# A two-layer mixer kernel: the narrow projection panel between the two halves of z, and its small products ahead of the head sums

## The reference, cut to what matters

```
n = rms_norm(h, norm_mix[l])
q, k, v, z, a, b, bq, bk, bv, iq, ik, iw = split(n @ w_in[l])      # 3408 columns
q, k, v = silu(causal_dwconv(q, k, v))
q = l2_norm(q) * 128 ** -0.5 ; k = l2_norm(k)                       # 4 heads of 128
g = -exp(a_log) * softplus(a + dt_bias) ; beta = sigmoid(b)
# chunked gated delta rule: decays from cumsum(g), one triangular solve per chunk
o = rms_norm(o, norm_g) * silu(z)
# second branch: bq, bk, bv attend to keys chosen by an indexer made of iq, ik (64 wide) and iw (8 wide)
ik = rope(rms_norm(ik))
```

## Time and profile before

| | |
|---|---|
| median of three runs | 1634.32 us (1628.2 to 1634.47) |
| profiled execution | 1631.81 us, its span 1630.0 us |
| mean granted clock of PE | 0.99 of full speed |
| busy share of the span | PE 97%, DVE 72%, ACT 56%, POOL 4% |
| shares of the chain that ended last | PE 82%, DVE 10%, ACT 4%, issue 2%, DMA 2% |
| the piece of the change, layer 0 | about 64 to 98 us |
| the piece of the change, layer 1 | about 527 to 558 us |

### The profile page before, as it was taken

How to read it: one execution, slowest core, us unless ns; L and a number is a source line. 1 busy time by engine, 2 the same in 40 slices (tenths; PEclk the granted TensorE clock), 3 DMA queues, 4 the chain that set the end, 5 groups by cost and what they waited for, 6 DMA issues and landing times.

```text
span 1630.0 us, 34719 instructions
## 1 busy us (share of the span) xinstructions
PE 1584.6 (97%) x12673; PEld 1546.5 (95%) x12673; DVE 1178.5 (72%) x1929; ACT 905.0 (56%) x1419; POOL 71.2 (4%) x62
## 2 busy tenths in 40 slices
PE   8997999999999989999999999999999999999998
PEld 7987989999999879899999989999999999999998
DVE  8778777866559689688666668888756746678863
ACT  5764465655446745556555555665645455566642
POOL 3101001000010101000000000000000000000000
PEclk9999999999999999999999999999999999999999
DMA  6643235455555432265665554566655544546663
GB/s 208 202 118 95 92 103 180 157 178 180 165 174 156 143 102 93 71 207 170 210 201 178 163 182 129 156 200 186 182 181 187 168 134 151 181 151 196 187 184 113
DMA packets 272207, 261.41 MB, mean 160 GB/s; under 512 B 20009, under 2 KB 270533, under 8 KB 272115
## 3 DMA queue, kind: packets, MB, share of 16 engines
q1 hardware_dynamic: 270547, 256.15, 50.9%
q0 software_dynamic: 1376, 3.87, 0.8%
q10 hardware_dynamic: 192, 0.14, 0.0%
HBM read 256.70 MB, written 3.42 MB: 160 GB/s over the span
## 4 chain that ended last, share of the span: by engine, by line
PE 82%; DVE 10%; ACT 4%; issue 2%; DMA 2%; SPq 1%; DVEq 0%; ACTq 0%
PE lin L551 22%; PE lin L554 22%; PE lin L559 22%; PE aux L899 6%; PE lin L899 3%; PE lin L605 3%; DVE wL L538 2%; PE lin L576 1%; ACT wH L529 1%; PE lin L636 1%; DVE cT L2075 1%; DMA stage<-in_w_gate 1%; DVE nT L2530 1%; DVE nL L2535 1%; DVE prod L2193 0%
## 5 line engine op out<-in xcount | busy, mean ns | idle before, releaser
L529 ACT ACTIVATE wH<-stage 128x1024 fp32r<-128x1024 f32 x488 | 493.5, 1049 | 479.8 <-PE lin L554 333.3
L538 DVE TENSOR_TENSOR wL<-stage,wH 128x1024 fp32r<-128x1024 f32 x488 | 580.2, 1231 | 141.1 <-PE lin L559 82.6
L551 PE MATMUL lin<-nH,wH 128*128 128x256 f32 (+2 forms) x2256 | 560.7, 287 | 3.3 <-DVE rawT L2146 2.4
L554 PE MATMUL lin<-nL,wH 128*128 128x256 f32 (+2 forms) x2256 | 555.4, 285 | 0.0
L551 PEld LDWEIGHTS lin<-nH,wH 128*128 128x128 f32 x2256 | 426.3, 189 | 6.8 <-issue 4.9
L554 PEld LDWEIGHTS lin<-nL,wH 128*128 128x128 f32 x2256 | 427.3, 189 | 1.1 <-issue 0.7
L559 PE MATMUL lin<-nH,wL 128*128 128x256 f32 (+2 forms) x2256 | 295.0, 283 | 0.5 <-DVE wL L538 0.5
L559 PEld LDWEIGHTS lin<-nH,wL 128*128 128x128 f32 x2256 | 281.4, 188 | 0.7 <-DVE wL L538 0.7
L551 PE MATMUL lin<-aH,wH 128*128 128x256 f32 (+1 forms) x704 | 172.3, 284 | 0.0
L554 PE MATMUL lin<-aL,wH 128*128 128x256 f32 (+1 forms) x704 | 172.2, 284 | 0.0
L551 PEld LDWEIGHTS lin<-aH,wH 128*128 128x128 f32 x704 | 132.8, 189 | 0.0
(11 more groups left out here) (416 smaller groups left out, 2200.9 us busy)
## 6 DMA issues: line engine op xcount, KB each, us to landing
stage<-in_w_up SPq DMA_DIRECT2D x88, 512.0 KB, 4.6
stage<-in_ffn_w_up SPq DMA_DIRECT2D x88, 512.0 KB, 4.3
stage<-in_w_in SPq DMA_DIRECT2D x52, 512.0 KB, 4.7
stage<-in_w_down SPq DMA_DIRECT2D x40, 512.0 KB, 3.7
stage<-in_ffn_w_down SPq DMA_DIRECT2D x40, 512.0 KB, 4.3
stage<-in_w_gate SPq DMA_DIRECT2D x32, 512.0 KB, 4.2
stage<-in_even_w_in SPq DMA_DIRECT2D x24, 512.0 KB, 4.6
stage<-in_w_out SPq DMA_DIRECT2D x16, 512.0 KB, 4.3
```

What stands on the lines that cost most here:

```text
L529: nc.scalar.activation(wH[:, s, ks, 0:n], stage[:, s, ks, 0:n], ACT.Copy).then_inc(sem["whi"], 1)
L538: nc.vector.tensor_tensor(wL[:, s, ks, 0:n], stage[:, s, ks, 0:n], wH[:, s, ks, 0:n].bitcast(F32), ALU.subtract).then_inc(sem["wlo"], 1)
L551: mm = nc.tensor.matmul(banks[b][0:rows_, 0:width], wH[:, s, k, cols], xh, start=start and n == 0, stop=False)
L554: mm = nc.tensor.matmul(banks[b][0:rows_, 0:width], wH[:, s, k, cols], xl, start=False, stop=False)
```

## The change

SP, ACT, DVE and PE take z's second half and the narrow panel in the other order: m0+4 slot 0 is z's first half, m0+4 slot 1 the narrow panel (PE writes bank 2 now), m0+5 slot 0 z's second half, m0+5 slot 1 the key panel as before. PE does `ta` and `sik` ahead of the eight head sums, behind z's second half. `JOBS` has the names in the new order. ACT copies the narrow panel between z's halves, and its `w_in(5, ...)` for z's second half begins with the split of panel m0+6 slot 0, whose place behind the `root`s is given up. `turned` on ACT stands in front of the `root_log`s.

```
--- before.py
+++ after.py
@@ -182,7 +182,7 @@
 
 
 JOBS = (
-    ["ms1"] + [f"ssq{h}" for h in range(4)] + ["ta"] + [f"ssk{h}" for h in range(4)] + ["sik", "gc", "tv"]
+    ["ms1", "ta", "sik"] + [f"ssq{h}" for h in range(4)] + [f"ssk{h}" for h in range(4)] + ["gc", "tv"]
     + ["gb0", "bb0", "gb1", "bb1"] + ["kk0", "qk0", "kk1", "qk1"] + ["gb2", "bb2", "kk2", "qk2"]
     + [f"ix0{e}" for e in range(2)] + [f"ix1{e}" for e in range(4)]
     + [f"sbq{h}" for h in range(4)] + ["sbk"] + ["Y1_4", "Y2_4"] + [x for b in range(3) for x in (f"kt{b}", f"vt{b}")]
@@ -726,11 +726,12 @@
                 with sp.Fori(1 if l == 0 else 0, 3) as i:
                     for s in range(2):
                         load(sp, m0 + i, s, whole(w_in, l, DC, i * 512 + s * PANEL))
-                for i, col in ((3, C_IQ), (4, 3 * 512)):
-                    for s in range(2):
-                        load(sp, m0 + i, s, whole(w_in, l, DC, col + s * PANEL))
-                load(sp, m0 + 5, 0, [(k0, k0 + 4, w_in[:, l * DC + k0:l * DC + k0 + 4, C_IK:IN_COLS]) for k0 in (0, 4)], IN_COLS - C_IK)
-                sp.dma_start(stage[:, 0, :, IN_COLS - C_IK:NARROW], w_in[:, l * DC:(l + 1) * DC, C_AB:C_AB + 8]).then_inc(sem["ab_in"], 16)
+                for s in range(2):
+                    load(sp, m0 + 3, s, whole(w_in, l, DC, C_IQ + s * PANEL))
+                load(sp, m0 + 4, 0, whole(w_in, l, DC, 3 * 512))
+                load(sp, m0 + 4, 1, [(k0, k0 + 4, w_in[:, l * DC + k0:l * DC + k0 + 4, C_IK:IN_COLS]) for k0 in (0, 4)], IN_COLS - C_IK)
+                sp.dma_start(stage[:, 1, :, IN_COLS - C_IK:NARROW], w_in[:, l * DC:(l + 1) * DC, C_AB:C_AB + 8]).then_inc(sem["ab_in"], 16)
+                load(sp, m0 + 5, 0, whole(w_in, l, DC, 3 * 512 + PANEL))
                 load(sp, m0 + 5, 1, whole(w_in, l, DC, C_BK))
                 for s in range(2):
                     load(sp, m0 + 6, s, whole(w_in, l, DC, C_BQ + s * PANEL))
@@ -957,11 +958,12 @@
                 multiply_second(pe, m0 + 1, r0 + 1, halves(0, nH, nL), T,
                                 lambda pair: (sem["nh"], at("nh", l, pair + 1)), lambda pair: (sem["nl"], at("nl", l, pair + 1)))
                 w_in(1, 1)
-                for i in (2, 3, 4):
+                for i in (2, 3):
                     for s in range(2):
                         w_in(i, s)
-
-                multiply(pe, m0 + 5, 0, r0 + 5, [(0, slice(0, NARROW), [(k, nH[:, k, :], nL[:, k, :]) for k in range(DC)])], T, rows_=NARROW)
+                w_in(4, 0)
+                multiply(pe, m0 + 4, 1, r0 + 4, [(2, slice(0, NARROW), [(k, nH[:, k, :], nL[:, k, :]) for k in range(DC)])], T, rows_=NARROW)
+                w_in(5, 0)
                 pe.wait_ge(sem["par_in"], 2 * DEPTH)
                 pe.wait_ge(sem["sq_heads"], at("sq_heads", l, 2))
 
@@ -970,18 +972,18 @@
                         name = f"ss{'qk'[h // 4]}{h % 4}"
                         mm(begin(name, l)[:, 0:T], ones, sqh[:, h, :]).then_inc(filled(name), 1)
 
-                def turned(name, x, p0, n, free):
+                def turned(name, x, p0, n, free, rnd):
                     ps = begin(name, l)
-                    pe.wait_ge(free, r0 + 6)
+                    pe.wait_ge(free, rnd)
                     for b in range(3):
                         t = nc.tensor.transpose(ps[0:TB[b][1], b * n:(b + 1) * n], x[p0:p0 + n, tok(b)], ident[p0:p0 + n, p0:p0 + n])
                     t.then_inc(filled(name), 1)
 
-                head_squares(0)
-                turned("ta", iab, IDX_DIM, 16, lin_read[0])
-                head_squares(4)
+                turned("ta", iab, IDX_DIM, 16, lin_read[2], r0 + 5)
                 pe.wait_ge(sem["sq_ik"], at("sq_ik", l, 1))
                 mm(begin("sik", l)[:, 0:T], ones, sq_ik[:, :]).then_inc(filled("sik"), 1)
+                head_squares(0)
+                head_squares(4)
                 w_in(5, 1)
                 pe.wait_ge(sem["tables_in"], 32)
                 pe.wait_ge(sem["gt"], at("gt", l, 1))
@@ -990,7 +992,7 @@
                     n = TB[b][1]
                     t = mm(ps[0:n, 4 * b:4 * b + 4], const("upto", n, n), gg[0:n, b, :])
                 t.then_inc(filled("gc"), 1)
-                turned("tv", bvT, 0, P, lin_read[3])
+                turned("tv", bvT, 0, P, lin_read[3], r0 + 6)
 
                 def gate(i, slots=(0, 1)):
                     for s in slots:
@@ -1494,9 +1496,9 @@
 
                 act.preload_act_table_set(SILU)
 
-                def w_in(i, to, func=Copy, slots=(0, 1), n=T):
+                def w_in(i, to, func=Copy, slots=(0, 1), n=T, cols=PANEL):
                     for s in slots:
-                        split_hi(act, m0 + i + 1, s)
+                        split_hi(act, m0 + i + 1, s, n=cols)
                         act.wait_ge(sem["panel_done"], 2 * (m0 + i) + s + 3)
                         for c in range(2):
                             b = 2 * s + c
@@ -1534,16 +1536,21 @@
 
                 w_in(3, lambda b: rawT[:, 20 + b:21 + b, META:T], slots=(0,), n=SEQ)
                 queries_swapped(0)
-                w_in(3, lambda b: rawT[:, 20 + b:21 + b, META:T], slots=(1,), n=SEQ)
                 act.wait_ge(sem["ab_in"], at("ab_in", l, 16))
-                for s in range(2):
-                    split_hi(act, m0 + 5, s, n=PANEL if s else NARROW)
-                    act.wait_ge(sem["panel_done"], 2 * (m0 + 4) + s + 3)
-                    for b in range(2 * s, 2 * s + 2):
-                        f(zT[:, b, :], lin[b][:, 0:T], Silu).then_inc(lin_read[b], 1)
-                    if s == 0:
-                        group_silu(2)
-                        queries_swapped(1)
+                w_in(3, lambda b: rawT[:, 20 + b:21 + b, META:T], slots=(1,), n=SEQ, cols=NARROW)
+                w_in(4, lambda b: zT[:, b:b + 1, :], Silu, slots=(0,))
+                group_silu(2)
+                queries_swapped(1)
+                act.wait_ge(sem["panel_done"], 2 * (m0 + 4) + 4)
+                f(iab[IDX_DIM:NARROW, :], lin[2][IDX_DIM:NARROW, 0:T], Copy)
+                for p0 in (0, IDX_DIM):
+                    t = f(ikr[p0:p0 + IDX_DIM, :], lin[2][0:IDX_DIM, 0:T], Copy)
+                t.then_inc(lin_read[2], 1)
+                act.sem_inc(lin_read[3], 1)
+                split_hi(act, m0 + 5, 1)
+                act.wait_ge(lin_read[2], r0 + 5)
+                f(sq_ik[:, :], ikr[:, :], Square).then_inc(sem["sq_ik"], 1)
+                w_in(5, lambda b: zT[:, 2 + b:3 + b, :], Silu, slots=(0,))
                 act.preload_act_table_set(EXP_LN)
 
                 def root_log(names, to, scale, h0=0):
@@ -1555,24 +1562,15 @@
                     act.wait_ge(*read(last, l))
                     f(to[:, :, :], to[:, :, :], Exp, scale=-0.5, bias=bias_).then_inc(sem["rn"], 1)
 
-                act.wait_ge(sem["panel_done"], 2 * (m0 + 5) + 3)
-                f(iab[IDX_DIM:NARROW, :], lin[0][IDX_DIM:NARROW, 0:T], Copy)
-                for p0 in (0, IDX_DIM):
-                    t = f(ikr[p0:p0 + IDX_DIM, :], lin[0][0:IDX_DIM, 0:T], Copy)
-                t.then_inc(lin_read[0], 1)
-                act.sem_inc(lin_read[1], 1)
-                act.wait_ge(lin_read[0], r0 + 6)
-                f(sq_ik[:, :], ikr[:, :], Square).then_inc(sem["sq_ik"], 1)
-                root_log([f"ssq{h}" for h in range(4)], rnq, 1.0)
-
                 def turned(name, to, n):
                     act.wait_ge(*full(name, l))
                     own.done(f(to[0:META, 0, :], bank(name)[0:META, 0:n], Copy))
                     f(to[:, 1:3, :], bank(name)[:, n:3 * n].rearrange("p (b n) -> p b n", b=2), Copy).then_inc(emptied(name), 1)
 
                 turned("ta", ab, 16)
+                root_log(["sik"], rni, 1.0 / P)
+                root_log([f"ssq{h}" for h in range(4)], rnq, 1.0)
                 root_log([f"ssk{h}" for h in range(4)], rnk, 1.0)
-                root_log(["sik"], rni, 1.0 / P)
                 act.wait_ge(sem["sp_in"], at("sp_in", l, 1))
                 own.done(f(gl[:, :, :], gm[:, :, :], Exp))
                 own.wait()
@@ -1581,7 +1579,6 @@
                 root("ssq3", rnq, lnq_col)
                 root("ssk3", rnk, 0.0)
                 root("sik", rni, 0.0)
-                split_hi(act, m0 + 6, 0)
                 act.wait_ge(sem["panel_done"], 2 * (m0 + 5) + 4)
                 for b, to in ((2, bkr), (3, bvT)):
                     f(to[:, :], lin[b][:, 0:T], Copy).then_inc(lin_read[b], 1)
@@ -2103,9 +2100,9 @@
                         ins = v.tensor_tensor(to[p0:p0 + 64], x[p1:p1 + 64], bf(table, 1, [64, x.shape[1], T]), ALU.mult)
                     ins.then_inc(sem["rope_sin"], 1)
 
-                for s in range(2):
-                    split_lo(dve, m0 + 4, s)
-                split_lo(dve, m0 + 5, 0, NARROW)
+                split_lo(dve, m0 + 4, 0)
+                split_lo(dve, m0 + 4, 1, NARROW)
+                split_lo(dve, m0 + 5, 0)
                 times_sin(0, iq_s[:, :, :])
                 split_lo(dve, m0 + 5, 1)
```

## The result

| | before | after |
|---|---|---|
| median | 1632.38 us (6 runs, 1628.2 to 1636.25) | 1639.58 us (6 runs, 1638.39 to 1641.12) |
| profiled execution | 1631.81 us, span 1630.0 us | 1638.39 us, span 1636.6 us |

The ratio is 1.0045, with a 95% interval of 1.0029 to 1.0062: 7.3 us slower, and outside of no change, though not by more than the 0.5% of the forecast's classes. A second series of the same kernel gave 1.0044 (1.0031 to 1.0057).

A forecast was written before the change was run, and what follows sets the result against it. TensorE (PE), busy 97% of the span, was taken as the bound, so only its standing time and half-clock time could change. 2.8 + 0.9 + 3.0 = 6.7 us slower gave 1640.5 us, range 1632 to 1646.

The forecast's parts named there:

- the sum: Key panel start 2.8 us later in layer 1, 0.9 in layer 0, plus 3.0 of slow clock: 6.7 us slower.
- The banks and what is late next: PE's wait at `ta` goes; `ssq2` waits for ACT's copy `ab`, some 2.8 us a layer, after 0.5 for `sq_ik`.
- ACT's list: ACT's work from reading z's first half to the end of copy `ab`, query split of 1.92 us included: 12.0 us.
- Where the list begins: ACT reads z's first half at 535.6 (layer 1) and 73.8 (layer 0), set by a 512 KB load landing in 4.7 us.
- that reading: By the 512 B rule, small loads were the bad ones; ACT would start no later than before, leaving 4.4 us.
- The clock: PE's clock falls during six sums behind its stop: 1.5 us lost a layer, bounds 0 and 2.7.
- The chain behind the key panel: From the key panel's end through ACT and DVE to the read of `Y`: its shift moves the layer's end equally.
- a sign against itself: Forecast is wrong if PE's wait for `Y` or `X` shrinks by what the key panel lost.
- What was set to nothing: Removing the 1.92 us query split before `bkr` gains nothing; PE's 0.6 us wait at z's second half, layer 0, is covered.
- No shift: The delay is absorbed because the inverse's chain starts elsewhere, say at DVE: 1634.3 us; chance 0.06.
- faster: ACT reaches `ta` before PE needs bank 1; standing and slow clock go: -3.5 us, 1630.8; chance 0.09.
- The slower one: Clock stays low for all six sums behind the stop at `ssq2`, both layers: 9.1 us slower, 1643.4; chance 0.23.

The follow-up runs named there:

- F: The changed kernel with ACT's copy of `ta` to `ab` moved ahead of the query panel's split and the table load; ratio to before 1.0065.
- B: The changed kernel with the query panel's first split put back behind the roots; ratio to before 1.0012, median 1634.14 us.
- J: The changed kernel with SP's key panel loads held until DVE has split the first half of z's second half; ratio to before 1.0041.
- H: The kernel before with the second half of the key panel's split moved behind the read of `ssk0`, both layers; ratio to before 1.0009.
- I: The kernel before with the second half of the key panel's split moved behind the read of `ssk0` in layer 0 alone; ratio 1.0002.

## Why the prediction was right, point by point

**Direction and size.** 1640.5 us was given and 1639.58 measured; by the ratio the change costs 7.3 us where the sum had 6.7. It fell in the forecast's own band (2.5 to 8.2 us), and the sum lies between what the stages lost in the two profiles, 4.7 us without a fall of the clock and 8.1 with one. That the absolute time came out within 1 us is in part luck: the base was put at 1633.8 (1640.5 - 6.7), and six runs gave 1632.38, while the sum was 0.6 too small. The range's lower end is not what its terms give: 1634.3 + 3.7 - 2 would be 1636, not 1632.

**The banks and what is late next: right.** The wait of `ta` went, and PE stood behind `ssq1` for `ab`, with the forecast wait for `sq_ik` in front. Forecast were 2.8 and 0.5 us, 3.3 together; measured were 2.38 and 0.85, 3.23 together, in both layers. F sharpens the step: the bank only names the wait, ACT's way to the end of the table load sets it.

**ACT's list: right to 0.2 us.** 12.0 us were summed from the read of z's first half to the end of `ab`; it took 549.71 - 537.87 = 11.84. That the query split is worth its full 1.92 us in it was shown by B (2.38 to 0.49).

**Where the list begins: mis-sized.** The forecast put ACT's read of z at 535.6 and 73.8, that is 9.9 and 11.0 us after the mark. It came 10.5 and 11.85 us after (537.87 - 527.35, 76.17 - 64.32). The term that was mis-sized is "a 512 KB load lands 4.7 us after its issue": the chain of waits shows 5.45 us for it in layer 0 and 5.20 in layer 1. The issue itself came within 0.1 us of the forecast (5.41 and 4.33 us after the mark; 5.33 and 4.26 were taken).

```profile
69.73 5.45 DMA stage<-in_w_in
...
531.68 5.20 DMA stage<-in_w_in
```

A median of seven loads was used for a single one. That is the difference in the stage: +0.9 was forecast for the start of the key panel in layer 0 and 1.7 measured (26.39 against 24.73 us from the mark), and +2.8 against 3.3 in layer 1. J did not show that the key panel's loads are what delays it; that is open. The page "DMA: Bandwidth & Descriptors" of the Trainium skill (Specifications), with its 512 B for full rate, was taken to say that ACT would start no later than before. ACT read z 2.4 us later in layer 1 (10.52 against 8.12 after the mark) and 1.4 in layer 0 (11.85 against 10.49), so that reading is out. The rule speaks of rate, and of rate the trace agrees: 144 KB in small pieces landed in a median of 3.0 us and 512 KB in 4.7, less than half the bytes per us. But the small load is over sooner all the same.

**The clock: right as a range, and luck in each execution.** 1.5 us a layer were taken, between 0 and 2.7. The four cases measured are 0 and 0 in one profile and 1.5 and 1.7 in the other. F, with nearly the same stops, kept the full clock in both layers, and J fell in both. So 1.5 us is what a fall costs, but it came in half of the cases, and "nearest to layer 0's" was too strong a reason for a fall in each: the same stops had none. The page "TensorE: Matmul & The Clock Gate" of the Trainium skill (What's actually happening) says that the moment of the change varies from run to run. The two profiles agree, and show more than that: a fall at one place or none.

**The chain behind the key panel: right, with one unlooked-for term.** In layer 1 the products of X started 3.2 us later after the mark (602.22 - 527.35 = 74.87 against 71.68), of the 3.3 us that the key panel had lost. In layer 0 they started 1.2 us later, of the 1.4 that the stage had lost. PE's next wait, for `Y`, was then shorter by 1.0 us, which the forecast had named as a sign against itself. What it waited for shows why, the chain of the kernel before, then after:

```profile
137.18 6.79 DMA stage<-in_w_gate
```

```profile
140.11 5.55 DMA stage<-in_w_gate
```

The gate's weights are issued 1.4 us later from the mark, as all else, and landed 1.2 us quicker in this execution. In layer 1 the same load took 5.82 us against 6.81, so that `Y` was read only 2.3 us later after the mark, not 3.3. In the second profile of the change it took 6.60 and 7.65 us, and `Y` was read 2.7 and 5.95 us later than before, where the stages had lost 2.9 and 5.1. So the shift was not absorbed by cover; a load happened to be quick.

**What was set to nothing.** Taking the split away ahead of `bkr` gave nothing: ACT's idle time there grew from 0.69 to 2.58 us. PE's wait for the read of z in layer 0 was 1.33 us rather than 0.6 and cost nothing, as ACT was later still. H shows the other side: 1 us of split put off into the same slack of 0.69 us made PE wait 1.1 us more, most of it by way of DVE and `gm`.

**The rivals.** No shift and faster are out by the interval of the ratio. The slower one (over 8.2 us) asked for 4.5 us of clock loss in the two layers; the second profile, whose span was 10.3 us above before's, had 3.2, and the first none. So one execution went this rival's way, but not that far, and the median did not.

## What to carry to other kernels

When small results go round a few banks, moving one ahead of the others moves the wait to the name that has its bank next; ask when the reading engine gets to its first read, not which name comes first. A helper that does two things (here the read of a panel and the split of the next) brings the second along when it is called earlier, and 1.9 us of split in front of a read cost PE 1.9 us of standing, while behind the `root`s they had been free: ACT idles 2.6 us there without them. Work that is put off on one engine can come back through another that follows it, as DVE's `gm` did in H. A single load on such a path should be given a range and not the median: the one that decided here took 5.20 to 6.75 us, where the median was 4.7.

## What was not expected of the hardware

Stops reproduced to 0.01 us between executions of the same kernel (2.38 and 0.85 us, both layers, both profiles), while the clock behind them fell in one and not in the other, which cost 1.5 and 1.7 us. In each of the four profiles with such stops (the change twice, F, J) both layers fell or neither did; why is open. A stage shorter by 2.0 us in one layer (I) did not show in the median of twelve runs, whose times spread over 8 us (1627.33 to 1635.51). And the load of the gate's weights in layer 0 took from 5.35 to 6.92 us to land over the twelve profiles.
